# Two chained transformer blocks on one core: expert weights stored and fetched by kind in 4 MB transfers, the order of work at the feed-forward borders, and extra products ahead of the convolution

## The reference, cut to what matters

```python
for l in range(2):                                  # first block
    h = h + 0.5 * rmsnorm(swiglu(rmsnorm(h), ffn1_gate_up, ffn1_down))     # width 2816
    h = h + rmsnorm(mixer(rmsnorm(h) @ w_in) @ w_out)   # HGRN2, window attention, spatial gating
    h = h + 0.5 * rmsnorm(swiglu(rmsnorm(h), ffn2_gate_up, ffn2_down))
    h = h + rmsnorm((p[l] @ ple_proj) * sigmoid(rmsnorm(h) @ ple_gate))    # per-layer embedding
h = concat([meta_tokens, h])                        # second block: 16 + 256 rows
h = h + short_conv_mixer(rmsnorm(h)); h = h + hier_moe(rmsnorm(h))         # layer 0
h = h + mla_mixer(rmsnorm(h), ...);   h = h + hier_moe(rmsnorm(h))         # layer 1
out = rmsnorm(h)[:, 16:]

def hier_moe(x):            # each row goes to the 2 best of the 64 experts, by group and within it
    for e in range(64):
        y[rows of e] += weight * ((silu(x @ w_gate[e]) * (x @ w_up[e])) @ w_down[e])   # 1024 -> 256 -> 1024
```

## Times and profile before

| | us |
|---|---|
| median of 3 runs | 2373.58 (2372.71 to 2374.41) |
| the profiled execution's own time | 2370.78 |
| its span | 2369.0 |
| PE busy | 2186.3 (92% of the span) |
| DVE busy | 1080.7 (46%) |
| mean granted clock of TensorE | 0.975 of full |
| read from HBM | 616.94 MB, 261 GB/s over the span |

### The profile page before, as it was taken

How to read it: one execution, slowest core, us unless ns; L and a number is a source line. 1 busy time by engine, 2 the same in 40 slices (tenths; PEclk the granted TensorE clock), 3 DMA queues, 4 the chain that set the end, 5 groups by cost and what they waited for, 6 DMA issues and landing times.

```text
span 2369.0 us, 27951 instructions
## 1 busy us (share of the span) xinstructions
PE 2186.3 (92%) x10672; PEld 1324.2 (56%) x10672; DVE 1080.7 (46%) x2074; ACT 384.0 (16%) x917; POOL 54.3 (2%) x95
## 2 busy tenths in 40 slices
PE   8999999999999999999999999888999998777776
PEld 7865558854885555884585544343437543333332
DVE  6665647665765665666322433233333343222222
ACT  2211331102210232110301210000003220000001
POOL 1200000000100000000000000000000000000000
PEclk9999999999999999999999999999999999898989
DMA  9542435532953334533592799999997289999998
GB/s 337 190 176 89 160 105 174 202 111 97 301 177 143 125 132 135 171 149 111 167 328 107 295 413 409 417 422 422 422 414 280 107 328 412 416 422 422 422 421 330
DMA packets 223561, 619.39 MB, mean 261 GB/s; under 512 B 16813, under 2 KB 122102, under 8 KB 179558
## 3 DMA queue, kind: packets, MB, share of 16 engines
q1 hardware_dynamic: 216400, 610.26, 67.4%
q0 software_dynamic: 1600, 5.06, 0.6%
q10 hardware_dynamic: 5462, 2.72, 0.4%
HBM read 616.94 MB, written 1.05 MB: 261 GB/s over the span
## 4 chain that ended last, share of the span: by engine, by line
PE 66%; DMA 19%; SPq 9%; DVE 2%; ACT 1%; issue 1%; DVEq 0%; POOL 0%; POOLq 0%; ACTq 0%
PE PS L2787 22%; DMA ring<-expert_parts 19%; PE PS L2870 11%; PE PS L1846 5%; SPq L1133 5%; PE PS L1739 4%; PE PS L2974 3%; PE PS L2928 3%; PE PS L3115 2%; SPq L1130 2%; SPq L1114 1%; PE PS L1799 1%; PE PS L865 1%; PE PS L1310 1%; PE PS L2957 1%
## 5 line engine op out<-in xcount | busy, mean ns | idle before, releaser
L1846 PE MATMUL PS<-ring,arena 128*32 128x512 f32 x1728 | 241.5, 692 | 117.7 <-DMA ring<-expert_parts 115.0
L2787 PE MATMUL PS<-ring,xT 128*128 128x256 f32 x1056 | 243.1, 379 | 3.5 <-ACT xT L2074 3.5
L2787 PEld LDWEIGHTS PS<-ring,xT 128*128 128x128 f32 x1056 | 200.2, 190 | 31.2 <-ACT xT L2074 4.2
L1799 PE MATMUL PS<-arena,xn 128*128 128x128 f32 x1280 | 203.2, 297 | 13.0 <-DVE h L1645 13.0
L1846 PEld LDWEIGHTS PS<-ring,arena 128*32 128x32 f32 x1728 | 64.1, 124 | 266.7 <-issue 239.1
L1799 PEld LDWEIGHTS PS<-arena,xn 128*128 128x128 f32 x1280 | 164.0, 189 | 73.1 <-issue 41.3
L2787 PE MATMUL PS<-arena,xn 128*128 128x256 f32 x704 | 165.7, 379 | 0.0
L1652 DVE TENSOR_TENSOR arena<-PS,small 128x512 f32<-128x512 f32 x62 | 42.8, 691 | 269.0 <-PE PS L1799 269.0
L2870 PE MATMUL PS<-ring,arena 128*128 128x512 f32 x352 | 162.8, 592 | 0.0
L2787 PEld LDWEIGHTS PS<-arena,xn 128*128 128x128 f32 x704 | 130.6, 190 | 16.1
L1815 PE MATMUL PS<-arena 128*128 128x512 f32 (+1 forms) x300 | 138.4, 603 | 0.0
(11 more groups left out here) (433 smaller groups left out, 2886.5 us busy)
## 6 DMA issues: line engine op xcount, KB each, us to landing
ring<-expert_parts SPq DMA_DIRECT2D x316, 1024.0 KB, 18.9
ring<-ffn_gate_up SPq DMA_DIRECT2D x88, 1024.0 KB, 10.4
ring<-ffn_down SPq DMA_DIRECT2D x44, 1024.0 KB, 7.3
arena<-expert_parts SPq DMA_DIRECT2D x73, 256.0 KB, 12.3
arena<-expert_parts SPq DMA_DIRECT2D x13, 1024.0 KB, 13.4
ring<-w_in SPq DMA_DIRECT2D x16, 768.0 KB, 6.0
ring<-conv_w_in SPq DMA_DIRECT2D x12, 1024.0 KB, 12.7
ring<-expert_parts SPq DMA_DIRECT2D x16, 512.0 KB, 15.2
```

Of the source, the lines that this page charges most:

```text
L1799: last = mm(PS[:, bank, at * P:(at + 1) * P], lhsT=xn[0:w, t, k * P:(k + 1) * P], rhs=onehot[0:w, t, :], start=t == 0, stop=t == nt - 1)
L1846: last = mm(PS[BLK * j:BLK * (j + 1), 2, :], lhsT=xgT[:, k, j * BLK:(j + 1) * BLK], rhs=w[k % HALF], start=k == 0, stop=k == KD - 1)
L2787: last = mm(out, lhsT=a[:, k, :], rhs=b[:, 256 * k:256 * (k + 1)], start=k == 0, stop=k == 3)
```

## The change

Expert parts stand in HBM as [layer, kind, partition, expert, 2048], and the ring is one row of 12 parts, kind by kind. Four neighbouring parts of one kind are then 32 KB in one piece in each partition, at both ends, and a quad is one transfer of 4 MB (`ring_load`). In HBM the pieces of two neighbouring partitions lie 64 x 8 KB = 512 KB apart. The groups up to `STATIC` = 14 are fetched in their natural order without the list; only groups 14 and 15 and any beyond use the list and parts of 1 MB. The extra places are `WHOLE` (four parts in one piece each), `BITS` (four parts of pieces, used once) and one or two alone, used once; `WRITTEN` is 7 and 3. In the places that are used once, neighbouring pieces go in one transfer.

At the borders ahead of the feed-forward layers 1 to 3, tile 0 is transposed before the last product of the sublayer ahead, ACT copies it sooner, and the first half of unit 1's first products stands before and around the transposes of tile 1. In `ple` each slot is freed by a drain of its own when its last product is done, and ACT squares a result before it takes the next gate. At the conv entry, six products of constants follow the meta rows' transposes and two the last transposes.

```diff
-    return np.ascontiguousarray(np.concatenate([gu, dn], 2))
+    return np.ascontiguousarray(np.concatenate([gu, dn], 2).transpose(0, 2, 3, 1, 4))
...
-        CYCLE = [RING[0] + RING[1] + RING[2] + [MORE[0], AHEAD[3]] + SPARE[3 - i:] + SPARE[:2]
-                 + [AHEAD[1], AHEAD[2], MORE[1], AHEAD[0], ROUTING] for i in (0, 1)]
...
+        def ring_parts(n, j0, j1):
+
+            return ringf[:, (GROUP * n + j0) * PART:(GROUP * n + j1) * PART]
...
+        BITS = [Place(const[:, LEVELS_AT:LEVELS_AT + 1024], sgw[:, :, :].rearrange("p g t -> p (g t)"), arena[:, 10944:11456]),
+                Place(mixed_rows[:, 0:1024], const[:, LEVELS_AT - 512:LEVELS_AT], rowsf[:, 3072:3584]),
+                Place(rowsf[:, 3584:4096], arena[:, 0:512], arena[:, 5424:5936], arena[:, 6192:6704]),
+                Place(arena[:, 13760:15296], arena[:, 15552:16064])]
+        META_ROWS = Place(h[:, 2, :], xn[:, 2, :])
+        ROUTING = Place(arena[:, 576:576 + PART])
+        ALONE = [[ROUTING], [META_ROWS, ROUTING]]
+        WRITTEN = (7, 3)
...
+        STATIC = NE // GROUP - 2
+
+        def quad(i, g, n):
+
+            q = 3 * g + n
+            if g >= WRITTEN[i] or q < 3:
+                return RING[n]
+            if q < 5:
+                return (WHOLE, BITS)[q - 3]
+            return (RING + [WHOLE])[(q - 5) % 4]
...
+            if (g, n) == (1, 2) and j < len(ALONE[i]):
+                return ALONE[i][j]
+            return quad(i, g, n)[j]
...
+        def parts_of(i, n, e, count):
+
+            return A["expert_parts"][i, n][:, bass.ds(e, count), :].rearrange("p e w -> p (e w)")
+
+        def ring_load(sp, i, g, n, j0=0, j1=GROUP):
+
+            loaded = signal_of(i, g, n)
+            place = RING.index(quad(i, g, n))
+            return sp.dma_start(ring_parts(place, j0, j1), parts_of(i, n, g * GROUP + j0, j1 - j0)).then_inc(loaded, 16)
...
+            for q in range(5, 3 * WRITTEN[i] + 3):
+                g, n = q // 3, q % 3
+                before = max(p for p in range(q) if quad(i, p // 3, p % 3) is quad(i, g, n))
+                part_used(before // 3, before % 3)
+                if q == 5:
+                    ring_load(sp, i, 1, 2, len(ALONE[i]), GROUP)
                     sp.wait_ge(S.routed, i + 1)
+                    place_load(sp, i, 1, 2, len(ALONE[i]) - 1)
+                elif quad(i, g, n) is WHOLE:
+                    for j in range(GROUP):
+                        place_load(sp, i, g, n, j)
+                else:
+                    ring_load(sp, i, g, n)
...
+            with sp.Fori(WRITTEN[i] + 1, STATIC) as g:
+                for n, loaded in enumerate((gu_loaded[i][0], gu_loaded[i][1], M[i].dn_loaded)):
...
+                    sp.dma_start(ring_parts(n, 0, GROUP), parts_of(i, n, g * GROUP, GROUP)).then_inc(loaded, 16)
...
+            with sp.Fori(STATIC, final) as g:
...
+                for _ in range({2: 6, 4: 2}.get(u, 0)):
+                    mm(PS[:, 5, 0:2 * P], lhsT=ident, rhs=const[:, 0:2 * P], start=True, stop=True)
...
+                if listed:
+                    pe.wait_ge(loaded, g * 64)
+                else:
+                    pe.wait_ge(loaded, g * 16 + max(SURPLUS[i][n], 0))
...
+                    if u == 2:
+                        h_copied(4 * l + 2, 64 * l + 32, FIRST_TILE)
...
                 gated(0)
+                squared(0)
                 gated(1)
-                squared(0)
+                squared(1)
                 gated(2)
-                squared(1)
+                if l + 1 < DEPTH:
+                    h_copied(4 * (l + 1), 64 * (l + 1), FIRST_TILE)
+                squared(2)
                 gated(3)
-                squared(2)
                 squared(3)
 
...
                     if u == 0:
-                        if turn:
-                            tile_turn(q, 0)
                         pe.wait_ge(S.xT_act, 3 * q + 1)
-                    part_arrived(pe, l, u0, 2 * u)
-                    product(PS[:, x, 0:256], a11, b11, done if u else None)
-                    if u == 0:
-                        if turn:
-                            tile_turn(q, 1)
-                        pe.wait_ge(S.xT_act, 3 * q + 2)
-                    product(PS[:, x, 256:512], a12, b21).then_inc(S.prod_done, 1)
+                    if u != 1 or m == 0:
+                        part_arrived(pe, l, u0, 2 * u)
+                        product(PS[:, x, 0:256], a11, b11, done if u else None)
+                        if u == 0:
+                            pe.wait_ge(S.xT_act, 3 * q + 2)
+                        product(PS[:, x, 256:512], a12, b21).then_inc(S.prod_done, 1)
+                    if u == 0 and m:
+                        second, next_ = X_BANK[1], part_of(u0, 2)
+                        part_arrived(pe, l, u0, 2)
+                        product(PS[:, second, 0:256], a11, next_[:, 0:1024])
+                        tile_turn(q, 1)
+                        product(PS[:, second, 256:512], a12, next_[:, 1024:2048])
                     if n == 0:
                         pe.wait_ge(S.rows_ready, 4 * m + 4)
                         part_arrived(pe, l, u0, 1)
...
+                    last = product(PS[:, z_, 256:512], a22, t4)
+                    if u == 1 and m:
+                        last.then_inc(S.prod_done, 1)
...
-                for n in range(2):
-                    mixed(1, n, (0, 1, 6, 7)).then_inc(S.y_done, 1)
+                mixed(1, 0, (0, 1, 6, 7)).then_inc(S.y_done, 1)
+                tile_turn(4 * l + 2, 0)
+                mixed(1, 1, (0, 1, 6, 7)).then_inc(S.y_done, 1)
...
                     last.then_inc(S.proj_done, 1)
+                    pe.drain().then_inc(unit_free[slot], 1)
...
+                        if t == i == 1 and l + 1 < DEPTH:
+                            tile_turn(4 * (l + 1), 0)
                         slot = (U_PLE + 1 + i) % SLOTS
                         dense(slot, slot_w(slot, KD, 512), 2 * t + i, t, 512).then_inc(S.gate_done, 1)
-                for i in range(3):
-                    pe.drain().then_inc(unit_free[(U_PLE + i) % SLOTS], 1)
+                        if t:
+                            pe.drain().then_inc(unit_free[slot], 1)
 
```

More of the change, by code:

```diff
@@ L619, in signal_of, with loads_of @@
             return (gu_loaded[i][0], gu_loaded[i][1], M[i].dn_loaded)[n]
+        def loads_of(i, g, n):
+            if g == 0:
+                return 2
+            if (g, n) == (1, 2):
+                return 1 + sum(len(v.pieces) for v in ALONE[i])
+            v = quad(i, g, n)
+            return 1 if v in RING else sum(len(u.pieces) for u in v)
         def landed_tables():
@@ L1938, in moe_pe @@
                     pe.sem_inc((gu_loaded[i][0], gu_loaded[i][1], M[i].dn_loaded)[n], -SURPLUS[i][n])
+            with pe.Fori(WRITTEN[i], STATIC) as g:
+                group(g, False)
+            for n in range(3):
+                pe.sem_inc((gu_loaded[i][0], gu_loaded[i][1], M[i].dn_loaded)[n], (64 - 16) * (STATIC - 1) - max(SURPLUS[i][n], 0))
             pe.wait_ge(S.routed, i + 1)
```

274 lines of the change are left out of this document (120 added, 154 removed).

## The result

The changed kernel takes 2348.39 us (median of 4 runs, 2347.71 to 2349.15), the kernel before 2373.14 in the same job (4 runs): a ratio of 0.9901, 95% interval 0.9888 to 0.9914. The profiled execution took 2347.72 us, its span 2345.9 for 2369.0.

What follows compares the result with a forecast made beforehand. DMA was taken to bound the mixtures, PE's waits the first block. Long rows 16.3, small pieces 5.5, borders 3.5 - 1.0, conv entry 2.0, places -2 gave 24.3 us saved: 2349 us, own range 2342 to 2356, wider range 2341 to 2379.

Steps and rivals of the forecast that it cites:

- Cost per packet: In DMA transfers: each packet costs an engine about 9.0 ns beyond its bytes, fitted from two stretches with engines never resting.
- Long rows: In the mixtures: 67 quads as single transfers with 32 KB rows save 0.243 us each, 16.3 us in all.
- the earlier start passes on whole: At the mixtures' start: time gained earlier is kept in full, since the first fetches there wait for PE.
- Small pieces: In the mixtures: 96 transfers of 256 KB replaced by whole parts at 8 KB rows, 5.5 us saved.
- Places: At the mixtures' start: fewer places from quad 9 on, margins of 1 to 2 us twice; cost 0 to 5, taken 2.
- too few places: Rival: quads land several us late at both mixtures' start and wherever PE is behind; 10 us lost, 2359 us, chance 0.09.
- Borders: At three feed-forward borders: earlier transposes remove PE's waits for ACT's copy, 2 x 0.80 + 1.86 = 3.5 us gained.
- drains: In the embedding: two more drains of PE a layer with work behind them, 4 x 0.25 = 1.0 us lost.
- the slots given back early buy nothing: In the embedding: freeing weight slots early gains nothing, as PE has no wait on a weight slot worth a row.
- Conv entry: At the conv entry: constant products in PE's holes keep the clock up, net 2.0 us gained, -0.7 if not.
- Cut rows: Rival: engines cut 32 KB rows into 8 KB, or cost is per byte; groups stay 29.8 us, 2365 us, chance 0.14.
- Row pitch: Rival: 512 KB between HBM pieces slows expert transfers; near 418 GB/s 2374 us, chance 0.09; 2391 and up, 0.13.

Runs made afterwards that it cites:

- experiment 4: Changed kernel with each full quad fetched in four transfers of every fourth partition, rows of 32 KB; 2347.18 us, ratio 0.9895 to the kernel before.
- experiment 1: Changed kernel with each full quad fetched by four transfers of 1 MB, rows of 8 KB, new HBM order kept; 2360.88 us, ratio 0.9954 to the kernel before.
- experiment 9: Changed kernel with quad 9 of layer 0 put into the fifth set of places, in pieces; 2346.68 us, ratio 0.9894 to the kernel before.
- experiment 10: Changed kernel with the old feed-forward borders and ACT's old order of copies and squares; 2351.66 us, ratio 0.9909 to the kernel before.
- experiment 7: Changed kernel with the four whole places filled in transfers of 256 KB again; 2351.57 us, ratio 0.9905 to the kernel before.
- experiment 6: Changed kernel with a pitch of 520 KB between partitions' expert rows in HBM instead of 512 KB; 2348.01 us, ratio 0.9898 to the kernel before.
- experiment 5: Changed kernel with a pitch of 2 MB between partitions' expert rows in HBM instead of 512 KB; 2443.88 us, ratio 1.0310 to the kernel before.

## Why the prediction was right, and where its terms were not

The forecast was 2349.0 us and 24.3 us saved; measured are 2348.39 and 24.8. The mechanism was right, but that the sum came out within 0.6 us is in part luck. In the profiles the two mixtures gave 6.9 and 9.3 us, 16.2 in all, where the forecast had 19.8 for them (and "about 11 us shorter each"). Against this stand 2.8 us in places that nobody changed.

- **Cost per packet.** Right. The fit of 9.0 ns from two stretches foretold 29.1 us a group and 432 GB/s; both came (29.14, and 430 to 432). The page has 43,800 packets fewer, where the forecast said some 30,000 and had left the pieces out. Per quad 0.23 us for 0.243. One detail was wrong: it charged the 3 closing packets that go as well, and experiment 4 shows these to be free, so that a row packet costs about 0.23 / 24 = 9.6 ns.
- **Long rows, 16.3 us.** Mis-sized: 12.5 (experiment 1), 12.4 by the groups. The failing step is the count, 67 quads, with the sentence that the earlier start passes on whole. Quads fetched before PE's first wait paid with idle engines for want of a place.
- **Small pieces, 5.5 us.** Mis-sized, probably for the same reason: 3.2 by the medians, 1.6 to 4.0 by the stage.
- **Places, -2 us.** The margins of 1 to 2 us were the right ones to look at. One place more lets the engines move 1.8 us' worth of bytes more up to 1480 us (experiment 9). The forecast's sign of the rival of too few places came, a share under 1 in the first 80 us of a mixture, and with it what its signs of being right had excluded, a stretch near 401 GB/s after 1360 us (402, at a share of 0.96). This cost and the two above are one thing seen twice: faster quads meet the same places.
- **Borders, 3.5 us, and drains, -1.0.** Right together: from PE's first transposes to the conv the changed kernel takes 1165.7 us for 1167.9, 2.2 us for 2.5. The waits removed are 3.7 us by experiment 10. The step "the slots given back early buy nothing" failed: with the new borders they hide a wait of 2.06 us. The forecast looked for PE's waits on weights alone; DVE's wait of 1.74 us stood in the trace of before, covered by ACT's of 1.86.
- **Conv entry, 2.0 us.** 1.64 in the profile, 1.4 by the medians; the clock is 1.00 from 1165 to 1180 us.
- **What the sum lacks.** The medians of the experiments would name 12.5 + 3.2 + 3.3 + 1.9 + 1.4 = 22.3 of 24.8 us, but they may not be added: the early slots earn their share only beside the new borders. With the 2.2 us that the two gave together in place of 3.3 + 1.9, 19.3 us are named and 5.5 stay open. For them I can name only chance (the medians' scatter; start and attention in the profiles). In layer 1 the kernel of experiment 1, with full quads fetched as before, still needs 2.3 us less than the kernel before (464.8 and 467.0 us from the router to the end), and small pieces cost nothing that shows there (experiment 7); but kernels that are the same in this stage differ by 3.3 us. The single terms are known to 1 or 2 us each at best.
- **The rivals.** Cut rows: no, one packet each. Too few places: real, at about a fifth of its price (1.8 for 10 us). Row pitch: no cost at 512 KB (experiment 6), though it exists at 2 MB (experiment 5); its 0.22 was the largest doubt, and the estimate of 2377 by the Trainium skill's rule (DMA: Bandwidth & Descriptors, Latency and other measured facts) was 28 us off here.

## What to carry to other kernels

Where the DMA engines are full, write packets and bytes of two unlike stretches as two equations; what a longer row saves follows before it is built. Then count only the transfers after the consumer's first wait: earlier savings come back as idle engines unless a place is free for them, so look at the DMA share in the stretches ahead of that wait. When a wait is removed, look in the trace for the waits of the other engines that it covered, on the weights of the next unit above all: they cost nothing before, and may afterwards.

## What the runs showed of the hardware

Quads fetched in four transfers of 32 neighbouring partitions keep all 16 engines at a share of 1.01 and move 210 GB/s; the same bytes in transfers of every fourth partition move 432. Rows of 8, 16 and 32 KB gave 422, 429 and 432 GB/s at full queue, 9.5 to 9.6 ns for each row packet per engine. Closing packets cost nothing that shows (1315 or 324 in 200 us, groups 29.14 us apart in both). A pitch of 2 MB between partitions slows transfers of 8 KB rows to 308 GB/s at a share of 1.01, where a pitch of 512 KB has 417, and leaves 32 KB rows at 432. The same hole of 1.93 us in PE's work is followed by a spell at half of its clock in ten profiles and not in four others, worth 1.7 us; behind the last quad, with holes of 2.8 us, the spell came in three profiles of eight that had such a hole.
